# One residual-and-norm hand-over chained, and the differential attention re-staged: query tiles computed inside it, probabilities joined and transposed one step behind their scores and multiplied with v two behind

## The chip, the cores and the metric

The kernel runs on one core of a Trainium2 chip. The metric is the time of one execution on the device in microseconds (us). Before the change three runs took 3192.56, 3198.44 and 3200.86 us; the median is 3198.44.

## The reference, cut to what matters

Two models run one after the other on 512 tokens of width 1024. The first has two layers (gated linear attention, then S5), each closed by an output projection added to `x`, and ends in a norm. The second puts 16 meta tokens in front (528 tokens, `L2`) and has an even layer (RWKV beside pooling), an MLP, an odd layer (differential attention) and an MLP. Two places matter here.

The seam between the models: `x = rms_norm(x, final_norm_w)` on the 512 tokens, and at once `h = rmsnorm([meta; x], norm_g_2[0][0])` on all 528, which feeds the even layer's input projection. `x` itself stays the residual.

The differential attention has 8 heads. Each head has two components c = 0, 1 of 64 dimensions and a value of 128. Rotary embedding is applied to q and k. Then:

```
s_c = causal(q_c k_c^T / 8),  p_c = softmax(s_c)           c = 0, 1
o   = (p_0 - lam * p_1) v          lam from four 64-vectors
o   = rms(o over 128) * subln * (1 - LAM_INIT),  then od_out
```

The last 512 tokens are queries, all 528 are keys.

## The kernel before, in words

Nothing is scheduled by a planner. Each stage is an object with methods `tensor`, `scalar`, `vector` and `gpsimd`, and each engine runs the stages' methods in the order in which they are appended; semaphores alone tie the engines together. The order of instructions on each engine is thus the order of the code.

Matrix products with weights (`Gemm`, L101) stream units of 128 x 1024 weights through a ring of four slots, loaded by SyncE. ScalarE rounds a unit to `high` (L362), GpSimd subtracts it from the unit to give the rest, `ring_r` (L353), and TensorE makes three products per 128 x 128 block: high weight by high input (L260), high by rest (L263), rest by high (L265). An output tile of 512 tokens is 24 matmuls of 512 columns; one of 528 tokens is 48 of 264.

The seam. `Rms` after out1 (built at L3183) gathers squares of `x` while out1 runs (`square` L512 on ScalarE, `add` L525 on VectorE), sums them over partitions with `ones` (L562, L566), takes the root (L547) and its reciprocal (L584), and scales `x` in place (L592). The second `Rms` (`pre(0, 0, rms)`, L3286) squares the new `x` tile by tile (L542), sums with 32 matmuls (L572), takes root and reciprocal again, writes `h` (L592), its rounding (L553) and its rest (L597); the first product of ev_a waits for the first rest. `RwkvPrepare` and `Rwkv` follow; in `Rwkv` GpSimd does only L2191.

The odd layer. `LateRms` (L609) lets the first output tile of the following product run in plain fp32 on unnormalised input (L246) and brings the statistic later. Then come, one after the other, all 8 query tiles (`RopeProjection`, 512 tokens), all 8 key tiles (528 tokens), `TokenInverse`, the values `gv` (four token tiles of 128 and one of 16), and `DiffAttention` (L2498). Rotary work per tile: four ScalarE copies of 32 rows (L2461, L2462), then three VectorE operations (L2491, L2493, L2495).

`DiffAttention` walks 32 steps n = (head h, query tile tau), with 144, 272, 400 or 528 keys. Its engines run:

- TensorE: scores of n for both components into banks 2(n%2) and 2(n%2)+1 (L2553, L2554; the 16 keys beyond 512 by L2552, L2557), then step n-2's probabilities transposed and combined as `prob_c x diag_c`, two accumulating fp32 products per key tile (L2568), then step n-3's product with v (L2579). All are fp32, and each such matmul appears in the trace as two passes.
- VectorE: adds the mask on the edge tile (L2672), one maximum for both components (L2677); for n-1 the inverse sums (L2691, L2692) and two diagonal matrices 1/sum_0 and lam/sum_1 (L2693, L2694).
- ScalarE: two exponentials with their sums (L2604, L2607), the copy of the transposed probabilities of n-2 (L2617, L2618); once per head the copy of the output (L2625) and four squares (L2639).

A tail makes the norm: root (L2642), diagonal spreads (L2702), products that transpose the output (L2589), its rounding (L2647) and rest (L2706), which feed od_out.

Of the kernel before, what the change touches and what calls it, by code (L numbers as in the profile page):

```python
# [23 lines left out]
P = 128  # L24
D = 1024
# [75 lines left out]
class Gemm(Stage):  # L101
# [13 lines left out]
    def __init__(self, b, name, kind, x, kt, outs, ranges, store, engines, needs, tiles=None, before=None,  # L115
# [10 lines left out]
        self.first_use = {}  # L126
        self.late, plain = late, int(late is not None)
# [28 lines left out]
        if high is not None:  # L156
            assert self.body_units % 2 == 0, name
            b.splits += self.body_units * self.iters - plain
# [48 lines left out]
    def tensor(self, pe):  # L207
# [26 lines left out]
        def one_out(o, it, ks=range(self.kt)):  # L234
# [5 lines left out]
            for c in range(ks[0] // 8, -(-(ks[-1] + 1) // 8)):  # L240
                w = self.unit(pe, it, o * self.per_out + c)
                for k in range(max(8 * c, ks[0]), min(8 * c + 8, ks[-1] + 1)):
# [12 lines left out]
                    if self.high is not None:  # L255
                        if self.ready and o == 0 and isinstance(it, int) and it == 0:
                            pe.wait_ge(*self.ready(k))
                        cols, hi = slice(k % 8 * P, (k % 8 + 1) * P), self.high[:, (o * self.per_out + c) % 2, :]
# [18 lines left out]
        def token_major(it):  # L277
            for j in range(self.body_units):
                w = self.unit(pe, it, j).rearrange("p (k n) -> p k n", k=2)
                for i, (t0, tn) in enumerate(self.tiles):  # L280
                    if j == 0:
                        free(i, it)
                    for kk in range(2):
                        if self.high is not None:
                            hi = self.high[:, j % 2, kk * 512:kk * 512 + 512]
# [63 lines left out]
    def make_low(self, eng, j, it):  # L349

        b, slot = self.b, (self.unit0 + j) % RING
        eng.wait_ge(b.unit_hi, self.split0 + j + 1 + it * self.body_units)
        eng.tensor_tensor(b.ring_r[:, slot, :], b.ring[:, slot, :], self.high[:, j % 2, :],  # L353
                                  ALU.subtract).then_inc(b.unit_lo, 1)

    def make_high(self, act, j, it, free=False):
# [5 lines left out]
        b.nc.scalar.activation(self.high[:, j % 2, :], b.ring[:, u % RING, :], ACT.Copy).then_inc(b.unit_hi, 1)  # L362
# [245 lines left out]

class LateRms(Stage):  # L609
# [79 lines left out]
class TokenInverse(Stage):  # L689


    def __init__(self, b, late, bank, to, turned, kept, before):
        self.b, self.late, self.bank, self.to = b, late, bank, to
        self.turned, self.kept, self.before = turned, kept, before

    def tensor(self, pe):
        b = self.b
        pe.wait_ge(*self.late.inverted)
        for o, (t0, tn) in enumerate(TOK_TILES):
            ins = b.nc.tensor.matmul(b.ps[0:tn, self.bank, o:o + 1], b.inv[:, t0:t0 + tn], b.ident[:, 0:1],  # L700
                                     start=True, stop=True)
        ins.then_inc(self.turned, 1)

    def scalar(self, act):
        act.wait_ge(self.kept, self.before + 2)

    def vector(self, dve):
        n = len(TOK_TILES) - 1
        tn = TOK_TILES[n][1]
        dve.wait_ge(self.turned, self.before + 1)  # L710
        self.b.nc.vector.tensor_copy(self.to[:, 0:n], self.b.ps[:, self.bank, 0:n]).then_inc(self.kept, 1)
        self.b.nc.vector.tensor_copy(self.to[0:tn, n:n + 1], self.b.ps[0:tn, self.bank, n:n + 1]).then_inc(self.kept, 1)
        dve.wait_ge(self.kept, self.before + 2)

# [958 lines left out]
N_CHUNKS = -(-L2 // RW_C)  # L1673
RANGES2 = HALVES
# [185 lines left out]
class Rwkv(Stage):  # L1860
# [323 lines left out]
    def gpsimd(self, pool):  # L2184
        b, m = self.b, self.m
        self.pool.gpsimd_tiles(pool)
        for n in range(self.groups):
            half, nch = n % 2, self.chunks(n // 2)
# [220 lines left out]
class RopeProjection(Stage):  # L2409


    def __init__(self, b, m, g, first, following, sems):
        self.b, self.m, self.g, self.first, self.following = b, m, g, first, following
# [3 lines left out]
        self.done = (self.done_, first + self.tiles)  # L2417
        self.kept = slice(META if len(g.ranges) == 1 else 0, L2)
        self.scale = 0.125 if first == 0 else 1.0
# [13 lines left out]
    def turn(self, n):  # L2433

        return self.m.part[(self.first + n) % 2]
# [14 lines left out]
    def shift(self, act, n):  # L2450

        b, at = self.b, self.first + n
# [12 lines left out]
    def scalar(self, act):  # L2465
# [9 lines left out]
        for n in (self.tiles - 2, self.tiles - 1):  # L2475
            self.shift(act, n)

    def vector(self, dve):
        b, m, v = self.b, self.m, self.b.nc.vector
        if self.first == 0:  # L2480
# [4 lines left out]
        for n in range(self.tiles):  # L2485
            at = self.first + n
            par, full = self.full(n)
            x, t = self.shaped(m.qk(at)), self.shaped(self.turn(n))
            dve.wait_ge(b.filled[par], full)
            dve.wait_ge(self.shifted, at + 1)  # L2490
            v.scalar_tensor_tensor(out=x, in0=self.source(n), scalar=self.scale, in1=cos, op0=ALU.mult,  # L2491
                                   op1=ALU.mult).then_inc(b.stored[par], 1)
            b.chain.link(v.tensor_tensor(t, t, sin, ALU.mult))  # L2493
            dve.wait_ge(b.stored[par], full)
            v.tensor_tensor(x, x, t, ALU.add).then_inc(self.done_, 1)  # L2495


class DiffAttention(Stage):  # L2498
# [4 lines left out]
    def __init__(self, b, m, needs):  # L2503
        self.b, self.m, self.needs = b, m, needs
        self.products = b.sem("da_products")
        self.summed = b.sem("da_summed")
        self.exped = b.sem("da_exped")
        self.scored = b.sem("da_scored")
        self.tail_scored = b.sem("da_tail_scored")
        self.maxed = b.sem("da_maxed")  # L2510
        self.powered = b.sem("da_powered")
        self.scaled = b.sem("da_scaled")
# [3 lines left out]
        self.out_kept = b.sem("da_out_kept")  # L2516
        self.steps = DIFF_HEADS * 4
        self.at = dict(b.norms)
        b.norms["squared"] += self.steps
# [4 lines left out]
        self.feeds = None  # L2524

    def parts(self, n):

        h, tau = divmod(n, 4)
        t0 = META + tau * P
        tiles = [(i * P, P) for i in range(tau + 1)] + [((tau + 1) * P, META)]  # L2530
        return h, tau, slice(t0, t0 + P), t0 + P, tiles

    def tensor(self, pe):
        b, m, mm = self.b, self.m, self.b.nc.tensor.matmul
        for s, v in self.needs:
            pe.wait_ge(s, v)
        pe.wait_ge(self.products, 1)
        mm(b.ps[:, 7, 0:2], b.ones[0:DIFF_DIM, :], m.lam_prod[0:DIFF_DIM, :], start=True, stop=True).then_inc(self.summed, 1)
        for n in range(self.steps + 3):
            if n < self.steps:  # L2540
                h, tau, tok, nk, tiles = self.parts(n)
                main = min(nk, 512)
                if n >= 2:
                    pe.wait_ge(self.powered, 2 * n - 2)
                if nk > main and h:
                    pe.wait_ge(self.kept, 4 * h)
                q = [m.qk(h)[DIFF_DIM * c:DIFF_DIM * (c + 1), tok] for c in range(2)]
                k = [m.qk(8 + h)[DIFF_DIM * c:DIFF_DIM * (c + 1)] for c in range(2)]
                to = [b.ps[:, 2 * (n % 2) + c, 0:main] for c in range(2)]
                tail = [b.ps[:, 6, META * c:META * (c + 1)] for c in range(2)]  # L2550
                if nk > main:
                    mm(tail[0], q[0], k[0][:, main:nk], start=True, stop=True).then_inc(self.tail_scored, 1)  # L2552
                mm(to[0], q[0], k[0][:, 0:main], start=True, stop=True)  # L2553
                ins = mm(to[1], q[1], k[1][:, 0:main], start=True, stop=True)  # L2554
                if nk > main:
                    pe.wait_ge(self.tail_scored, h + 1)
                    ins = mm(tail[1], q[1], k[1][:, main:nk], start=True, stop=True)  # L2557
                ins.then_inc(self.scored, 1)
            if 2 <= n < self.steps + 2:
                j = n - 2  # L2560
                h, tau, tok, nk, tiles = self.parts(j)
                pe.wait_ge(self.scaled, j + 1)
                if j >= 2:
                    pe.wait_ge(self.kept, j - 1)
                for i, (k0, kn) in enumerate(tiles):
                    to = b.ps[0:kn, 4 + j % 2, i * P:(i + 1) * P] if i < 4 else b.ps[0:kn, 6, P:2 * P]
# [978 lines left out]
```

## Time and profile before

| what | value |
|---|---|
| median of three runs | 3198.44 us |
| the profiled execution's own time / its span | 3202.0 / 3200.2 us |
| granted TensorE clock over the span | 0.964 |
| TensorE matmul busy | 2927.9 us, 91% |
| VectorE / ScalarE / GpSimd busy | 1398.6 (44%) / 1008.2 (32%) / 1050.6 (33%) us |
| seam, last add to `x` until first product of ev_a | 1637.7 to 1664.8 us of the span |
| query / key / value products (after the late tile) | 2459.4 to 2506.6 / to 2553.9 / to 2611.0 |
| differential attention, first score to last product with v | 2612.8 to 2742.0 |

TensorE's busy share says little on its own, since its ends are modelled. What a change is worth is read from a stretch: its length, the starts of successive groups on TensorE, and the idle time in brackets with what ended it. The granted clock is 1.0 at 2.4 GHz and 0.5 at 1.2 GHz; a mean between them is a share of time at each.

### The profile page before, as it was taken

To read this page: it belongs to the slowest core of one execution; us is meant where nothing else is said; L and a number is where in the kernel's file an instruction comes from. 1 tells how busy PE (TensorE), PEld (TensorE's weight loads), DVE (VectorE), ACT (ScalarE), POOL (GpSimd) and SP (SyncE) were. 2 spreads that over 40 slices of the span, in tenths; PEclk is the share of its full clock that TensorE was granted. 3 is DMA by queue.
4 is the path that set the end of the run, shared out by engine and by line. 5 is a ranking of instruction groups with operands and counts; after the bars stand their busy time and mean duration, and the time that the engine had idled before them with its cause. 6 is when DMAs were issued, how large, how long until landed. Compare 5 with 4: busy or idle time off the path is not lost. (4 is left out here: it accounts for less than half of the span.)

```text
span 3200.2 us, 45703 instructions
## 1 busy us (share of the span) xinstructions
PE 2927.9 (91%) x18218; PEld 2384.0 (74%) x18218; DVE 1398.6 (44%) x2300; ACT 1008.2 (32%) x1613; POOL 1050.6 (33%) x725
## 2 busy tenths in 40 slices
PE   6898789899899899898979888899998999989997
PEld 4666467677688578786768876799997867768885
DVE  5787254510206511302038575380634425283352
ACT  2222264222312235423225332311124525431121
POOL 0332022444323169444433300144442320234442
PEclk9999899999999899999999997999999999999999
DMA  3898011144472269322222100122222210122222
GB/s 138 259 273 260 22 46 47 59 154 155 150 210 92 80 159 257 117 94 77 93 77 67 41 3 15 60 89 89 93 91 75 86 46 1 47 73 98 92 96 75
DMA packets 130754, 324.91 MB, mean 102 GB/s; under 512 B 54144, under 2 KB 54784, under 8 KB 129808
## 3 DMA queue, kind: packets, MB, share of 16 engines
q1 hardware_dynamic: 96128, 221.90, 21.5%
q0 software_dynamic: 30096, 88.21, 9.8%
q10 hardware_dynamic: 4352, 12.25, 1.0%
q8 instruction: 133, 2.18, 0.3%
q14 instruction: 45, 0.37, 0.0%
HBM read 288.32 MB, written 33.95 MB: 101 GB/s over the span
## 5 line engine op out<-in xcount | busy, mean ns | idle before, releaser
L353 POOL TENSOR_TENSOR ring_r<-ring,high 128x1024 fp32r<-128x1024 f32 x327 | 823.5, 2518 | 1570.6 <-ACT high L362 1570.5
L260 PE MATMUL ps<-h_hi,high 128*128 128x512 f32 (+1 forms) x2112 | 737.8, 358 | 55.0 <-POOL ring_r L353 23.7
L265 PE MATMUL ps<-h_hi,ring_r 128*128 128x512 f32 (+1 forms) x2112 | 663.2, 349 | 0.0
L263 PE MATMUL ps<-h_r,high 128*128 128x512 f32 (+1 forms) x1920 | 646.2, 346 | 0.0
L362 ACT ACTIVATE high<-ring 128x1024 fp32r<-128x1024 f32 x359 | 379.5, 1057 | 831.0 <-PE ps L260 711.0
L260 PEld LDWEIGHTS ps<-h_hi,high 128*128 128x128 f32 x2112 | 402.7, 191 | 133.9 <-issue 61.6
L265 PEld LDWEIGHTS ps<-h_hi,ring_r 128*128 128x128 f32 x2112 | 372.3, 191 | 53.6
L263 PEld LDWEIGHTS ps<-h_r,high 128*128 128x128 f32 x1920 | 367.7, 192 | 42.1 <-issue 1.7
L263 PE MATMUL ps<-f_r,high 128*128 128x264 f32 (+1 forms) x832 | 261.2, 326 | 0.0
L260 PE MATMUL ps<-f_hi,high 128*128 128x264 f32 (+1 forms) x768 | 236.6, 321 | 0.0
L260 PE MATMUL ps<-z_hi,high 128*128 128x512 f32 x488 | 196.6, 403 | 16.7 <-POOL ring_r L353 10.9
L265 PE MATMUL ps<-f_hi,ring_r 128*128 128x264 f32 (+1 forms) x768 | 205.0, 321 | 0.0
L265 PE MATMUL ps<-z_hi,ring_r 128*128 128x512 f32 x488 | 192.4, 394 | 0.0
L263 PEld LDWEIGHTS ps<-f_r,high 128*128 128x128 f32 x832 | 156.8, 188 | 14.4
L2920 ACT ACTIVATE arena<-ps 128x512 f32<-128x512 f32 (+4 forms) x102 | 58.3, 575 | 342.1 <-PE ps L265 251.8
L260 PEld LDWEIGHTS ps<-f_hi,high 128*128 128x128 f32 x768 | 144.4, 188 | 11.4
L263 PE MATMUL ps<-z_lo,high 128*128 128x512 f32 x360 | 145.4, 404 | 0.0
L265 PEld LDWEIGHTS ps<-f_hi,ring_r 128*128 128x128 f32 x768 | 127.0, 188 | 11.0
L3354 DVE CAST f_hi<-f x64 | 131.6, 2056 | 7.8
L260 PEld LDWEIGHTS ps<-z_hi,high 128*128 128x128 f32 x488 | 92.9, 190 | 44.9 <-issue 14.5
L263 PE MATMUL ps<-z_hi,high 128*128 128x512 f32 x280 | 112.5, 402 | 0.0
L265 PEld LDWEIGHTS ps<-z_hi,ring_r 128*128 128x128 f32 x488 | 93.2, 191 | 22.4
(430 smaller groups left out, 4387.6 us busy)
## 6 DMA issues: line engine op xcount, KB each, us to landing
ring<-in_units SPq DMA_DIRECT2D x402, 512.0 KB, 3.3
d_ca<-arena POOLq DMA_DIRECT2D x16, 640.0 KB, 8.7
arena<-d_ca POOLq DMA_DIRECT2D x16, 640.0 KB, 6.0
arena<-d_q POOLq DMA_DIRECT2D x32, 256.0 KB, 7.8
d_pb<-arena POOLq DMA_DIRECT2D x16, 512.0 KB, 10.5
arena<-d_pb POOLq DMA_DIRECT2D x16, 512.0 KB, 4.0
arena<-d_ca POOLq DMA_DIRECT2D x16, 512.0 KB, 5.1
arena<-d_k POOLq DMA_DIRECT2D x128, 64.0 KB, 4.4
```

The source lines that it names most:

```text
L260: part = mm(acc, hi[:, cols], self.x_hi(k)[:, t0:t0 + tn], start=(k == 0), stop=False)
L263: mm(acc, hi[:, cols], self.x(k)[:, t0:t0 + tn], start=False, stop=False)
L265: ins = mm(acc, w[:, cols], self.x_hi(k)[:, t0:t0 + tn], start=False, stop=(k == self.kt - 1))
L353: eng.tensor_tensor(b.ring_r[:, slot, :], b.ring[:, slot, :], self.high[:, j % 2, :], ALU.subtract).then_inc(b.unit_lo, 1)
L362: b.nc.scalar.activation(self.high[:, j % 2, :], b.ring[:, u % RING, :], ACT.Copy).then_inc(b.unit_hi, 1)
L2920: return nc.scalar.activation(to, ps, ACT.Copy, scale=1.0 if scale is None else scale)
L3354: nc.vector.tensor_copy(hi, t).then_inc(mlp_parts, 1)
```

## The change

Seam. One stage `ChainedNorms` replaces both norms. While out1 runs, ScalarE squares each tile twice, plain and scaled by the weight w (with a scale column that `WideColumns` computes once, near the start), and VectorE adds both running sums. TensorE sums the meta tokens' squares and the weighted sums; one root and one reciprocal of these give the factor for `h`, since the second norm of a normed input is, up to its epsilon, a norm of `x * w`. The factor of the first norm is taken later from the plain sums, behind the `h` work, and `x` is brought up to date tile by tile by GpSimd inside `Rwkv`.

Odd layer. New order: 8 key tiles (late tile first), one query tile, `TokenInverse` with lam, values (16 meta tokens now last), then `DiffAttention` with the other 7 query tiles inside. Each step holds two of the eight k-blocks of a query tile, 6 matmuls (`query_tile`). In the attention:

- score bank c is used in every step; component c of step n waits for the exponential c of step n-1; the mask is a third accumulating matmul, `ident_r x hide_r`; the maximum is taken per component;
- `join`: VectorE computes `p_0 - (lam sum_0 / sum_1) p_1` unnormalised in one operation, TensorE transposes it once per key tile, one step behind the scores, and multiplies with v two behind;
- the division by sum_0 moves to the copy of the head's output, now VectorE's (`keep_out`); squares move to GpSimd and their sum to VectorE;
- GpSimd makes the 7 query units' rests, ScalarE their roundings and rotary copies, VectorE their rotary sums, all between attention steps.

Core of the diff (weights reordered to match, and buffers moved):

```diff
+    def scalar(self, act):                      # ChainedNorms
+        act.wait_ge(b.summed, at["summed"] + 1)
+        f(b.root[:, META:], b.ps[:, 0, :], ACT.Sqrt, bias=b.eps[self.eps * self.eps], scale=1.0 / self.width)
+        f(b.root[:, 0:META], b.ps[:, 2, 0:META], ACT.Sqrt, bias=b.eps[self.eps], scale=1.0 / self.width)
+        self.feeds.make_high(act, 0, 0)
...
+    def residual(self, pool, k):                # called by Rwkv.gpsimd before its wait for group k
+        pool.tensor_scalar(x, x, b.col("final_norm_w", k), 1.0, ALU.mult, ALU.mult).then_inc(b.normed, 1)
+        pool.wait_ge(b.normed, at["ready"] + self.n + 2 * k + 1)
+        pool.tensor_tensor(x, x, b.inv[:, META:], ALU.mult).then_inc(b.normed, 1)
...
     # DiffAttention.tensor, step n
-                mm(to[0], q[0], k[0][:, 0:main], start=True, stop=True)
-                ins = mm(to[1], q[1], k[1][:, 0:main], start=True, stop=True)
+                for c in range(2):
+                    to = b.ps[:, c, 0:main]
+                    if n:
+                        pe.wait_ge(self.powered, 2 * n - 1 + c)
+                    mm(to, q[c], k[c][:, first:nk], start=True, stop=False)
+                    mm(to[:, main - P:main], m.ident_r, m.hide_r, start=False, stop=True).then_inc(self.scored, 1)
+                self.query_tile(pe, 4 + 2 * n)
-                j = n - 2
-                pe.wait_ge(self.scaled, j + 1)
-                    for c in range(2):
-                        ins = mm(to, m.prob[:, j % 3, c, k0:k0 + kn], m.diag[:, j % 2, c, :], start=(c == 0), stop=(c == 1))
+                j = n - 1
+                pe.wait_ge(self.joined, j + 1)
+                    ins = b.nc.tensor.transpose(self.turned_to(j, i, kn), m.prob[:, j % 3, 0, k0:k0 + kn], b.ident[:, :])
-                j = n - 3                       # product with v
+                j = n - 2
...
+        def join(j):                            # vector, after the maxima of step j + 1
+            dve.wait_ge(self.powered, 2 * j + 2)
+            link(v.reciprocal(inv, tot))
+            link(ts(inv[:, 1:2], inv[:, 1:2], tot[:, 0:1], m.lam, ALU.mult, ALU.mult))
+            stt(out=p[:, 0], in0=p[:, 1], scalar=inv[:, 1:2], in1=p[:, 0], op0=ALU.mult, op1=ALU.add).then_inc(self.joined, 1)
...
+        for n in range(self.steps + 1):         # scalar
+            power(n); keep(n - 1)
+            if n % 4 == 0: self.q.g.high_unit(act, n // 4 + 1)
+            if n % 4 == 1 and n // 4 < self.q.tiles: self.q.shift(act, n // 4)
...
+        for h in range(DIFF_HEADS):             # gpsimd, after low_unit(0) and low_unit(1)
+            self.q.g.low_unit(pool, h + 2)
+            squares(h)
```

## Rows read from the trace of the kernel before

**Rows 1.** The page, busy time of each engine.
```profile
PE 2927.9 (91%) x18218; PEld 2384.0 (74%) x18218; DVE 1398.6 (44%) x2300; ACT 1008.2 (32%) x1613; POOL 1050.6 (33%) x725
```

**Rows 2.** By stretch: length, busy PE PEld DVE ACT POOL, granted clock, DMA, GB/s.
```profile
1820.00:1860.00 40.00, 34.10 (x995) 30.57 (x995) 21.86 (x59) 13.62 (x35) 3.31 (x3) 1.00 0.01 4
1085.00:1143.00 58.00, 43.56 (x132) 24.97 (x130) 22.93 (x74) 17.27 (x50) 6.76 (x12) 0.82 0.16 46
2459.40:2506.60 47.20, 42.73 (x175) 33.33 (x174) 32.45 (x37) 29.81 (x46) 17.79 (x7) 0.96 0.33 108
2506.60:2553.90 47.30, 46.92 (x385) 46.74 (x384) 18.50 (x25) 27.71 (x40) 19.38 (x8) 1.00 0.28 90
2553.90:2611.00 57.10, 56.84 (x251) 41.39 (x250) 5.43 (x10) 13.14 (x16) 16.81 (x7) 1.00 0.22 74
2612.80:2742.00 129.20, 125.97 (x834) 93.31 (x834) 68.87 (x227) 69.22 (x289) 0.00 (x0) 0.97 0.01 1
```

**Rows 3.** Timeline of the seam: start, us, engine, line, operation, [idle before <-releaser].
```profile
1637.71 1.07 DVE L3173 TENSOR_TENSOR x<-x,ps 128x512 f32<-128x512 f32 x1 [15.07 <-PE ps L265]
1638.70 0.68 DVE L525 TENSOR_TENSOR sq<-sq 128x512 f32<-128x512 f32 x1
...
1639.53 1.10 PE L562 MATMUL ps<-sq,c_ones 128*128 128x512 f32 x2 [1.85 <-DVE sq L525]
1640.46 1.02 PE L566 MATMUL ps<-sq,c_ones 128*128 128x512 f32 x2
1641.52 0.69 ACT L547 ACTIVATE root<-ps,c_eps 128x512 f32<-128x512 f32 x1 [0.77 <-PE ps L566]
...
1658.45 3.45 DVE L584 RECIPROCAL inv<-root 128x528 f32<-128x528 f32 x1 [7.43 <-ACT root L547]
...
1661.93 2.13 DVE L592 SCALAR_TENSOR_TENSOR h<-x,cols,inv 128x528 f32<-128x528 f32 x3
1664.83 0.56 PE L260 MATMUL ps<-h_hi,high 128*128 128x264 f32 x1 [7.30 <-DVE h_r L597]
```

**Rows 4.** Timeline of VectorE behind the seam, in `RwkvPrepare`.
```profile
1681.57 0.15 DVE L1689 TENSOR_SCALAR sq<-arena 128x1 f32<-128x1 f32 x1 [5.29 <-ACT arena L2920]
```

**Rows 5.** Timeline of one head of the attention, TensorE's groups and some of VectorE's.
```profile
2648.31 0.60 PE L2553 MATMUL ps<-arena 64*128 64x400 f32 x1
...
2653.81 1.22 DVE L2677 TENSOR_REDUCE arena<-ps 128x2 f32<-128x1024 f32 x1
...
2659.30 0.49 PE L2553 MATMUL ps<-arena 64*128 64x272 f32 x1
...
2659.97 2.59 PE L2568 MATMUL ps<-arena 128*128 128x128 f32 x20
...
2662.49 1.35 PE L2579 MATMUL ps<-arena 128*128 128x128 f32 x8
...
2663.76 0.60 PE L2553 MATMUL ps<-arena 64*128 64x400 f32 x1
```

**Rows 6.** Groups by line over that head, 2648.31 to 2663.76.
```profile
L2568 PE MATMUL ps<-arena 128*128 128x128 f32 (+1 forms) x56 | 7.7, 282 | 0.1
```

**Rows 7.** Timeline in `Rwkv`: transposes on TensorE, GpSimd's only work.
```profile
1834.83 1.09 PE L1969 MATMUL ps<-c_ident,arena 128*128 128x128 f32 x8
...
1835.51 1.27 POOL L2191 TENSOR_TENSOR arena<-arena,memn 128x512 f32<-128x512 f32 x1 [14.74 <-ACT arena L2084]
```

**Rows 8.** Timeline of a softmax step of the memory attention, TensorE.
```profile
1117.17 0.44 PE L761 MATMUL ps<-c_ident,p 128*128 128x128 f32 x2 [0.98 <-DVE p L797]
1117.44 1.03 PE L742 MATMUL ps<-arena 128*128 128x256 f32 x4
```

**Rows 9.** Timeline at the turn from queries to keys: VectorE and GpSimd.
```profile
2510.32 2.48 POOL L353 TENSOR_TENSOR ring_r<-ring,high 128x1024 fp32r<-128x1024 f32 x1 [5.27 <-ACT high L362]
2510.58 2.77 DVE L2495 TENSOR_TENSOR arena<-arena 128x512 f32<-128x512 f32 x1
```

**Rows 10.** Timeline of TensorE after the last product with v.
```profile
2746.73 3.78 PE L2589 MATMUL ps<-arena 128*128 128x128 f32 x16 [4.74 <-DVE arena L2702]
```

More of the change, by code:

```diff
@@ L704, in scalar @@
[L704 to L713 removed]
+        pe.wait_ge(*self.free)
@@ L1673 @@
 N_CHUNKS = -(-L2 // RW_C)
+KEY_TILES = [(META + t * P, P) for t in range(4)] + [(0, META)]
 RANGES2 = HALVES
@@ L2433, in turn @@
     def turn(self, n):
-        return self.m.part[(self.first + n) % 2]
+        return self.m.part[(self.base + n) % 2]
     def full(self, n):
@@ L2450, in shift @@
     def shift(self, act, n):
-        b, at = self.b, self.first + n
+        b, at = self.b, self.base + n
         par, full = self.full(n)
@@ L2474, in scalar @@
         self.following.make_high(act, 0, 0)
-        for n in (self.tiles - 2, self.tiles - 1):
+        for n in range(max(0, self.tiles - 2), self.tiles):
             self.shift(act, n)
@@ L2524, in __init__, with turned_to @@
         self.feeds = None
+        self.turned_at = turned.base - 1
     def parts(self, n):
         h, tau = divmod(n, 4)
-        t0 = META + tau * P
-        tiles = [(i * P, P) for i in range(tau + 1)] + [((tau + 1) * P, META)]
-        return h, tau, slice(t0, t0 + P), t0 + P, tiles
+        tiles = [(META + i * P, P) for i in range(tau + 1)] + [(0, META)]
+        return h, tau, META + tau * P, META + (tau + 1) * P, tiles
+    def turned_to(self, j, i, kn):
+        b = self.b
+        return b.ps[0:kn, 4 + j % 2, i * P:(i + 1) * P] if i < 4 else b.ps[0:kn, 6, P:2 * P]
@@ L2533, in tensor, with query_tile @@
+    def query_tile(self, pe, n):
+        if n < 8 * self.q.tiles:
+            it, o = divmod(n // 8, self.q.g.body_outs)
+            self.q.g.one_out(o, it, range(n % 8, n % 8 + 2))
     def tensor(self, pe):
         b, m, mm = self.b, self.m, self.b.nc.tensor.matmul
[L2535 to L2538, printed above, removed]
@@ L2611, in keep @@
         def keep(j):
-            h, tau, tok, nk, tiles = self.parts(j)
+            h, tau, t0, nk, tiles = self.parts(j)
             act.wait_ge(self.turned, j + 1)
@@ L2695, in vector @@
+        for n in range(self.steps + 4):
+            if n >= 6 and n % 4 == 2:
+                keep_out(n // 4 - 1)
+            if n < self.steps:
+                top(n)
+            if 1 <= n <= self.steps:
+                join(n - 1)
+            if n % 4 == 2 and n // 4 < self.q.tiles:
+                self.q.combine(dve, n // 4)
+            if n >= 8 and n % 4 == 1:
+                sum_squares(n // 4 - 2)
+        sum_squares(DIFF_HEADS - 1)
         dve.wait_ge(b.rooted, self.at["rooted"] + 1)
@@ L2984, in build @@
         stages.append(rms)
+        wide = Views()
+        columns = b.sb("wide", [P, 2, KD])
+        wide.scale, wide.gain = columns[:, 0, :], columns[:, 1, :]
+        wide.meta = b.h[:, 4, 0:KD * META].rearrange("p (k t) -> p k t", k=KD)
+        stages.append(WideColumns(b, wide))
         memn = lambda k: b.memn[:, k, :]
```

486 lines of the change are left out of this document (299 added, 187 removed).

## The prediction

> **What bounds the kernel now.** I read the page's busy line first: TensorE is busy 91%, no other engine half [rows 1]. So a part pays where it takes work off TensorE or shortens a stretch in which TensorE idles. Next the two stretches that the change touches. At the seam the timeline shows the last add to `x` starting at 1637.71 and the first product of ev_a at 1664.83; between them runs one chain over ScalarE and VectorE, twice (root, reciprocal, scaling), with TensorE only summing squares [rows 3]. In the odd layer, key and value products fill TensorE (46.92 of 47.30, 56.84 of 57.10 us); the query products, which come first, carry start-up losses (42.73 of 47.20); the attention takes 129.20 us with TensorE busy 125.97 [rows 2]. One head of the attention lasts 2663.76 - 2648.31 = 15.45 us [rows 5]. TensorE's program sets that pace; VectorE, ScalarE and GpSimd are busy 69, 69 and 0 of 129 us [rows 2].
>
> **The seam.** The last add ends at 1638.78. After it VectorE adds twice (two L525 of 0.68): 1640.15. TensorE sums the meta squares, 16 short passes; no row shows 16-column passes of this kind, the bounds are near 0 and the 0.12 of a 128-column pass, and since weights change each time I take 0.1: 1.7 us. The weighted sums take what L562 and L566 take now, 1639.53 to 1641.48, 1.95: 1643.8. Root 0.69, a small root and hand-overs 0.35: 1644.85. Reciprocal 3.45: 1648.3. From there the first product starts 1664.83 - 1661.93 = 2.90 after the reciprocal now; three tiles now need an extra 16-column instruction each, 0.1 apiece: 1651.5 [rows 3]. That is 13.3 earlier. The later tiles come every 1.42 instead of 1.30 us for seven tiles, 0.8 back: gain 12.4, bounds 10 and 14.
>
> What it pushes elsewhere: the reciprocal for `x` (3.4 us) stands on VectorE behind the `h` work, ahead of `RwkvPrepare`. VectorE waits 5.29 us there for ev_a's second tile [rows 4], which hides it; with that cover gone it would cost 3.4. The second square and add per tile run beside out1, whose tiles come over 15 us apart (the add waited 15.07) [rows 3]: nothing. The update of `x`, 8 times two GpSimd operations of some 1.27, goes where GpSimd idles 14.74 us between pieces [rows 7]; L2191 waits for ScalarE, not for GpSimd. It can hold up VectorE (see below), bounds 0 and 8 x 1.3 = 10; the operations of VectorE that follow L2191 mostly read PSUM, I take 0.
>
> **The odd layer outside the attention.** Two start-ups change hands. Query stage now: 7 tiles after the late one, 24 matmuls at 0.232 = 5.57 each, 39.0 of 47.2, so 8.2 of start-up loss. Keys run at 47.3/8 = 5.9 with none [rows 2]. After: 7 key tiles 41.1 + the same 8.2 = 49.3; one query tile 5.6; values 57.1 unchanged; a hand-over to the attention 0.7, since two query chunks (2.8 us) cover the constants. lam leaves the start of the attention.
>
> **TensorE's work per head.** Products with diagonals go: 56 passes [rows 6], 20 of them from 2659.97 to 2662.49 at 0.126: 7.1 us. In their place 14 transposes of one pass each. Eight transposes take 1.09 to the end of the last, and the last itself about 0.27: 0.117 apiece [rows 7], so 14 x 0.12 = 1.7. Products with v stay, 28 passes at 0.155 (the 8 from 2662.49 to 2663.76 at 0.159): 4.3 [rows 5].
>
> Scores become dearer. Now the two components use different halves of the array's rows and overlap: 272 columns take 2659.30 to 2659.97, 0.67, for four passes [rows 5]; by that slope the four query tiles of a head take about 3.05. The mask product, on all rows, now stands between c = 0 and c = 1, so they run one after the other. A pass alone: 256 columns on all rows, four in 1.03 [rows 8], 0.24 each, hence 0.15, 0.26, 0.36 and 0.46 for 144 to 512 columns; 16 passes 4.9. Bounds: 4.9, and 6.1 if each keeps its present pace. I take 4.9, the lone pass being the nearer kind. Meta scores 0.4. Masks: 8 products of 128 columns in fp32r; from a full-rate product (0.232 per 512 columns) 0.06, from a whole fp32 product of 128 columns, two passes, 0.25; I take 0.10, nearer the first since it is of that kind, 0.8 per head. Query chunks: 24 x 0.232 = 5.6. Sum with queries 4.9 + 0.4 + 0.8 + 5.6 + 1.7 + 4.3 = 17.7; without them 12.1.
>
> **Gaps on TensorE.** Transposes of n-1 wait for `join`, which VectorE starts only after both maxima of n. So after the scores of n, TensorE has 1.39 us of query chunk, and VectorE needs: hand-over 0.2; maximum of c = 1 (1024 columns take 1.22 [rows 5], so 0.28, 0.40, 0.53 and 0.65, with 0.2 more at tau = 3); two small operations 0.4 (three at a predecessor of 528 keys, 0.6); the joining operation over n-1's keys (528 columns about 0.77; 0.30, 0.45, 0.60 below); hand-over 0.06. Per tau 0 to 3: 1.91, 1.36, 1.64, 2.11, less 1.39: 0.52, 0, 0.25, 0.72.
>
> GpSimd adds one. It had nothing to do in the attention [rows 2]. A VectorE operation with both inputs in SBUF that begins under a GpSimd operation waits for its end: L2495 began 0.26 after a GpSimd start and took 2.77 in place of about 0.7, ending just behind it [rows 9]. By the order of ScalarE's program, rounding of the next query unit ends as step tau = 1 begins, GpSimd's 2.48 follow, and that step's join falls under them: its 0.30 becomes some 1.45, gap 1.12. The squares (1.27) fall under maxima, which read PSUM. Gaps per head: 0.52 + 1.12 + 0.25 + 0.72 = 2.6, a period of 20.3. ScalarE, some 10 us of it, follows.
>
> Head 8 and most of head 7 have no query chunks: 12.1 + 7.0 = 19.1. The whole: lead-in chunks 2.8, first head 16.1 (its first steps have nothing to transpose or multiply), five at 20.3, one at 19.2, the last with its drain 22.5: 162.1.
>
> **The clock.** In `Rwkv` TensorE is busy 34.1 of 40 and the grant is 1.00; in the memory attention, with 0.98 of idle in each step of about 2.3 us [rows 8], 43.56 of 58, it is 0.82 [rows 2]. The last ten steps (some 37 us) have such gaps. At 0.82, 13 us at half speed; TensorE is about 0.62 of the chain, half of that lost: 4 us. Bounds 0 and 15.
>
> The Trainium skill, page "TensorE: Matmul & The Clock Gate", Part 4, says that transpose-mode products don't count as activity for the clock gate. No row here isolates it: the memory attention has both gaps and transposes, `Rwkv` has transposes at a grant of 1.00. If so, the steps without queries would fall sooner; it makes the last rival likelier, and no term above hangs on it.
>
> **Tail.** Now 4.74 us from the last product with v to the next on TensorE [rows 10]. After: scaled copy 0.7, GpSimd squares 1.3, their sum 0.6, root 0.3, reciprocal 0.35, spread 0.7, hand-overs 0.4, 4.3 in all. I count it equal.
>
> **Sum.** Before, 2459.4 to 2742.0 is 282.6. After: 49.3 + 5.6 + 57.1 + 0.7 + 162.1 = 274.8, gain 7.8, less 4 for the clock 3.8. With the seam's 12.4: 16.2. The profiled execution took 3202.0 (span 3200.2), so 3185.8; it stands 3.6 above the median of 3198.4, so 3182.
>
> **Rivals.**
> - *Cheaper attention.* GpSimd doesn't hold up the join (0.87 + more per head, 6.5 in all), the clock holds (4), masks at 0.06 (2): 12.5 better, 3170. For: the attention's TensorE was steady at nearly 1.00. Against: rows 9.
> - *Scores at their present pace.* Each pass keeps 0.24 to 0.52 when alone, 1.2 per head, 7.3 with the knock-on, and masks 0.13 or more, 2 more: 3191. For: short passes carry weight loads. Against: [rows 8].
> - *Slower, the clock.* Gaps in every step, with short and transposing work between, bring the grant down through the whole attention. At the memory attention's 0.82 over 162 us, 58 us run at half speed; half of it lost, 29, less 4 counted: 3207. Fully at 1.2 GHz it would be over 100 more. It decides from 26 us lost. For: [rows 8] at 0.82. Against: query chunks of 1.39 us in 26 of 32 steps, and `Rwkv` at 1.00 with gaps.
> - *The norm hand-over is not worth it*, because VectorE bounds `RwkvPrepare` and starts late: 9 instead of 12.4, 3186; inside the forecast's range.
>
> **How the numbers follow.** A run can tell 0.3%, 9.6 us, from no change: faster is below 3188.8. Forecast 3182 has 0.52 (own range 3175 to 3190), cheaper attention 0.22, present-pace scores 0.16, the clock 0.10. Faster: nearly all of the first two less a tail, 0.69; same, the third and that tail, 0.21; slower 0.10. Range 3162 to 3200: the low end adds the seam's and chunks' upside to the second case, the high end leaves out the clock case.
>
> **What would show it.** Seam: ev_a's first product 13 us closer to the last add, one reciprocal in between. Attention: head period near 20.3 with query chunks and 19 without; transposes at 0.12; score passes of one component not overlapping the other's; the join at tau = 1 stretched under L353; grant near 1 until the last two heads. Wrong if the head period is above 22, if the seam gives under 9, or if VectorE's joins are never stretched.

## The result and the profile after

The changed kernel took 3217.44 us in the median (8 runs), the kernel before 3199.89 beside it: ratio 1.0049, 95% interval 1.0035 to 1.0063. It is slower by half a per cent, where 3182 was forecast with 3162 to 3200 as its range. The profiled execution took 3212.11 (span 3210.3) against 3202.0. One of the 8 runs, a stray of 7313.84 us that nothing here explains, counts in the median (3216.53 without it) but not in the ratio.

The page, busy time of each engine, answers to [rows 1]:

```profile
PE 2932.5 (91%) x17926; PEld 2370.7 (74%) x17926; DVE 1406.5 (44%) x2290; ACT 999.7 (31%) x1521; POOL 1075.2 (33%) x751
```

The trace has 292 passes of TensorE fewer (18218 to 17926) and TensorE is busy 4.6 us longer: the first sign that what was taken off it came back at a higher price. By stretch of the changed kernel (columns as in [rows 2]): `Rwkv`, keys, the first query tile, values, the attention, its last head:

```profile
1820.00:1860.00 40.00, 34.25 (x1004) 30.02 (x997) 26.42 (x67) 15.78 (x36) 9.16 (x9) 1.00 0.01 3
2449.10:2498.60 49.50, 44.95 (x350) 43.51 (x349) 35.53 (x38) 31.45 (x49) 17.31 (x7) 1.00 0.31 105
2498.60:2504.40 5.80, 5.80 (x33) 4.93 (x32) 4.11 (x3) 3.73 (x6) 2.52 (x1) 1.00 0.26 90
2504.40:2561.00 56.60, 56.60 (x246) 41.24 (x245) 5.48 (x12) 15.12 (x20) 19.19 (x8) 1.00 0.22 75
2562.70:2752.70 190.00, 173.47 (x717) 111.30 (x716) 89.34 (x227) 85.28 (x235) 21.54 (x13) 0.86 0.05 18
2713.90:2752.70 38.80, 32.08 (x94) 20.77 (x93) 11.50 (x31) 9.77 (x28) 1.04 (x1) 0.50 0.00 1
```

Keys, first query and values lie where the forecast put them (49.3, 5.6 and 57.1). The attention takes 190 us, and its last row shows a granted clock of 0.50, the lower of TensorE's two levels, 1.2 GHz.

The seam, timeline of the changed kernel, against [rows 3]:

```profile
1636.95 1.07 DVE L3364 TENSOR_TENSOR x<-x,ps 128x512 f32<-128x512 f32 x1 [15.05 <-PE ps L266]
...
1639.27 1.96 PE L661 MATMUL ps<-h,c_ones 128*128 128x16 f32 x16 [2.36 <-DVE sq L654]
...
1644.74 0.27 ACT L675 ACTIVATE root<-ps,c_eps 128x16 f32<-128x16 f32 x1
...
1645.04 3.45 DVE L690 RECIPROCAL inv<-root 128x528 f32<-128x528 f32 x1 [5.82 <-ACT root L675]
...
1651.81 0.56 PE L261 MATMUL ps<-h_hi,high 128*128 128x264 f32 x1 [5.35 <-DVE h_r L700]
```

One reciprocal stands between the last add and the first product; from the start of the one to the start of the other it is 14.86 us, before 27.12.

A steady head of the attention, TensorE's timeline of the changed kernel, step tau = 0 whole, of tau = 1 and 3 the part in question:

```profile
2645.77 0.51 PE L2727 MATMUL ps<-arena 64*128 64x144 f32 x2
2646.21 0.33 PE L2731 MATMUL ps<-z_hi 128*128 128x128 f32 x1
2646.47 0.51 PE L2727 MATMUL ps<-arena 64*128 64x144 f32 x2
2646.91 0.33 PE L2731 MATMUL ps<-z_hi 128*128 128x128 f32 x1
2647.07 0.45 PE L261 MATMUL ps<-h_hi,high 128*128 128x512 f32 x1
...
2648.29 0.39 PE L266 MATMUL ps<-h_hi,ring_r 128*128 128x512 f32 x1
2649.02 0.76 PE L2740 MATMUL ps<-c_ident,arena 128*128 128x128 f32 x5 [0.34 <-DVE arena L2867]
2649.62 1.25 PE L2750 MATMUL ps<-arena 128*128 128x128 f32 x8
2650.80 0.72 PE L2727 MATMUL ps<-arena 64*128 64x272 f32 x2
2651.45 0.33 PE L2731 MATMUL ps<-z_hi 128*128 128x128 f32 x1
...
2665.82 0.66 PE L2740 MATMUL ps<-c_ident,arena 128*128 128x128 f32 x4 [0.58 <-DVE arena L2867]
...
2667.27 0.39 PE L2727 MATMUL ps<-arena 64*128 64x144 f32 x1
```

Read the first five lines from start to start. Two passes of 144 columns for component 0 (0.44), their mask (0.26), two passes for component 1 (0.44), mask (0.16), and only then the query chunk: 1.30 us. In [rows 5] the two components' passes of 272 columns begin together, four in 0.67; here that tile takes 1.72 with its masks. Over the head the scoring blocks are 1.30, 1.72, 2.15 and 2.75, together 7.92 us.

The steps of head 8, which have no query chunk beside them:

```profile
2713.90 0.84 PE L2727 MATMUL ps<-arena 64*128 64x144 f32 x2
...
2718.11 1.33 PE L2740 MATMUL ps<-c_ident,arena 128*128 128x128 f32 x5 [1.78 <-DVE arena L2867]
2719.24 2.21 PE L2750 MATMUL ps<-arena 128*128 128x128 f32 x8
...
2744.06 1.12 PE L2740 MATMUL ps<-c_ident,arena 128*128 128x128 f32 x4 [2.03 <-DVE arena L2867]
...
2756.83 3.79 PE L2760 MATMUL ps<-arena 128*128 128x128 f32 x16 [4.09 <-DVE arena L2888]
```

The same passes take 0.84 where they took 0.51. The last line is the tail, 4.09 against 4.74 [rows 10].

### The profile page after: what moved, and what is told of

It is laid out like the page before. It is cut to its first block and busy times, and to the rows that moved or that the text cites. A ratio compares the mean times of both kernels' runs of the same rounds, so it can differ in the third digit from the quotient of the medians.

```text
span 3210.3 us, 45040 instructions
## 1 busy us (share of the span) xinstructions
PE 2932.5 (91%) x17926; PEld 2370.7 (74%) x17926; DVE 1406.5 (44%) x2290; ACT 999.7 (31%) x1521; POOL 1075.2 (33%) x751
## 3 DMA queue, kind: packets, MB, share of 16 engines
q8 instruction: 131, 2.15, 0.3%
## 5 line engine op out<-in xcount | busy, mean ns | idle before, releaser
L261 PEld LDWEIGHTS ps<-z_hi,high 128*128 128x128 f32 x488 | 93.0, 191 | 49.3 <-issue 14.0
L266 PEld LDWEIGHTS ps<-z_hi,ring_r 128*128 128x128 f32 x488 | 93.1, 191 | 22.3
## 6 DMA issues: line engine op xcount, KB each, us to landing
d_pb<-arena POOLq DMA_DIRECT2D x16, 512.0 KB, 10.7
```

The lines of the kernel that those rows point to most:

```text
L261: part = mm(acc, hi[:, cols], self.x_hi(k)[:, t0:t0 + tn], start=(k == 0), stop=False)
L266: ins = mm(acc, w[:, cols], self.x_hi(k)[:, t0:t0 + tn], start=False, stop=(k == self.kt - 1))
```

## The experiments

Times are medians, ratios are to the kernel before in the same call. "Attention" is measured within each profiled execution, from the first score to the end of the last product with v, so that nothing ahead of it moves it. "Period" is a steady head, from one 144-key score to the next; "head 7 / 8" are the last two heads, the eighth to its last product with v.

```
kernel            median   ratio (95%)             attention  period  head 7 / 8
changed           3217.44  1.0049 (1.0035-1.0063)    190.1    21.50   25.1 / 38.8
seam_only         3188.32  0.9963 (0.9949-0.9977)    129.2    15.46   15.5 / 24.5
odd_only          3218.51  1.0064 (1.0043-1.0086)    188.4    21.51   24.2 / 38.8
no_mask           3188.41  0.9962 (0.9943-0.9981)    166.1    19.42   21.1 / 32.2
filler            3195.90  0.9978 (0.9966-0.9989)    174.0    21.50   21.3 / 24.8
filler_turns      3192.59  0.9977 (0.9961-0.9992)    173.9    21.50   21.3 / 24.7
adjacent          3196.21  0.9979 (0.9964-0.9994)    172.6    19.98   22.8 / 33.6
adjacent_filler   3176.58  0.9920 (0.9896-0.9945)    160.2    19.98   20.1 / 23.9
join_first        3187.67  0.9968 (0.9956-0.9980)    167.2    19.50   17.6 / 32.5
pairs_and_join    3159.96  0.9876 (0.9858-0.9894)    142.0    17.03   16.9 / 26.6
all_three_six     3159.76  0.9881 (0.9861-0.9901)    140.6    17.03   16.9 / 25.3
all_three         3158.57  0.9865 (0.9841-0.9889)    137.9    17.03   17.1 / 22.4
```

**seam_only**: the kernel before with the new norm stage and nothing else of the change.

```diff
-        rms = pre(0, 0, rms)
+        rms = ChainedNorms(b, x2, KD, D, EPS, wide, lambda i: b.h[:, 5 + i, 0:L1], h_hi, h2_lo, h2)
...
+                self.norms.residual(pool, n)
```

> The kernel before with the new norm hand-over alone; the differential attention is the old one. Theory A (the seam saves what its steps saved, 13 us, and 3 to 4 of them go back at the end of Rwkv because the grant falls to 0.50 about 8 us earlier there, counted from the kernel's own place): -9 to -10 us, some 3190. Rival (the seam's 13 us stay whole): -12 to -13, some 3187. Rival (a lower clock eats them all): within 2 us of before. The attention must last as long as before, 293 us from the odd layer's late tile to the last v product.

It is 0.37% faster, 11.8 us of 3200 (the interval is 7.4 to 16.3; the medians differ by 12.6). The attention is as it was (129.2). By the times, Theory A and its first rival differ by 3 us and neither is excluded; that the clock eats the gain is.

The traces do tell them apart. This is the stretch of `Rwkv` at the lower clock, in the kernel before and in the changed one:

```profile
1952.90:1987.00 34.10, 28.53 (x239) 20.70 (x239) 17.64 (x60) 7.95 (x23) 0.91 (x2) 0.50 0.00 1
1932.00:1976.30 44.30, 37.67 (x403) 28.86 (x402) 23.02 (x79) 8.71 (x26) 0.91 (x2) 0.50 0.01 1
```

Counted from the last add to `x`, `Rwkv` begins 164.8 and 164.9 us later in the two kernels with the old norms, and 151.3 to 154.2 in the eleven with the new ones, the changed kernel among them: a lead of 10.6 to 13.6. From there to the late tile of the first MLP it is 253.2 with the old norms. In nine of the eleven it is 256.3 to 256.6, and in those the low stretch lasts 44 us, as here. In the two others (filler_turns, all_three_six) it lasts 34 us as before, and the distance is 253.1. So where the low stretch is longer 3.2 us of the lead go back, as Theory A has it; where it is not, nothing does, which also shows that the update of `x` on GpSimd costs nothing.

**odd_only**: the converse, the new odd layer behind the old norms.

```diff
-        stages.append(RopeProjection(b, m3, gq, 0, None, turns))
...
+        keys = Turned(b, m3, gk, 0, 0, None, turns)
...
-        da = DiffAttention(b, m3, [rope.done, third_in] + done(gv))
+        da = DiffAttention(b, m3, queries, done(gv))
```

> The changed odd layer alone, with the old norm hand-over. If the two parts add up: +21 to +25 us, some 3221 to 3225, and the same fall of the grant to 0.5 once the query chunks have run out, about 25 us before the last v product. If the loss in the attention came from the seam's shift of the clock, the grant stays at 1.0 through the attention here and the time is within 8 us of before.

Slower by 0.64% (0.43 to 0.86), 20.5 us; the attention is that of the changed kernel to 2 us, with the clock falling in the same place, in head 7 soon after the last query chunk. So the whole loss belongs to the odd layer. The two ratios give +0.27% together where the changed kernel has 0.49; each has an interval of 0.14 to 0.22 to either side, so they are not at odds.

**no_mask**: how much is the mask's place worth? The kernel leaves the causal mask out of the computation.

```diff
-                    mm(to, q[c], k[c][:, first:nk], start=True, stop=False)
...
-                    mm(to[:, main - P:main], m.ident_r, m.hide_r, start=False, stop=True).then_inc(self.scored, 1)
+                    mm(to, q[c], k[c][:, first:nk], start=True, stop=True).then_inc(self.scored, 1)
```

> The changed kernel without the mask product, so the scores above the diagonal stay unmasked (left out of the computation: the causal mask). Theory B (the full-row mask product between the two components' scores is what keeps them from running beside each other): the scoring blocks of a steady head fall from 7.9 us to 3.4 to 3.8, the period from 21.5 to about 17.5, and the time by 25 to 35 us against the changed kernel, some 3185. Rival (they run one after the other because each waits for its own component's exponentials): only the masks' own 1.7 us per head go, scoring 6.2, period about 19.8, -12 to -14 us, some 3204.

TensorE's timeline at tau = 0 and 1 of a steady head, with VectorE's and GpSimd's rows of tau = 1:

```profile
2656.18 0.52 PE L2729 MATMUL ps<-arena 64*128 64x144 f32 x4
2656.63 0.51 PE L261 MATMUL ps<-h_hi,high 128*128 128x512 f32 x1
...
2660.47 0.73 PE L2729 MATMUL ps<-arena 64*128 64x272 f32 x4
2661.26 2.38 POOL L354 TENSOR_TENSOR ring_r<-ring,high 128x1024 fp32r<-128x1024 f32 x1 [13.24 <-ACT high L363]
2662.43 1.37 DVE L2865 SCALAR_TENSOR_TENSOR arena<-arena 128x144 f32<-128x144 f32 x1
2663.86 0.44 PE L2738 MATMUL ps<-c_ident,arena 128*128 128x128 f32 x2 [1.07 <-DVE arena L2865]
```

Four passes of 144 columns now take 0.45 and the blocks of a head 3.71 in place of 7.92. Theory B is right about the pairs: they run side by side again, though each component still waits for its own exponentials, so those waits didn't part them. But the period falls by 2.1 and not by 4: TensorE waits 3.1 us a head for the join (0.40, 1.07, 0.47, 1.12) instead of 0.9. The time fell by 0.87%, 28 us, all the same, more than eight times 2.1. Of it the trace shows 24.0 in the attention, 10.7 of them in the last two heads, where the clock is low.

**adjacent**: the same products in another order.

```diff
                 for c in range(2):
...
-                    mm(to, q[c], k[c][:, first:nk], start=True, stop=False)
-                    mm(to[:, main - P:main], m.ident_r, m.hide_r, start=False, stop=True).then_inc(self.scored, 1)
+                    mm(to[c], q[c], k[c][:, first:nk], start=True, stop=False)
+                for c in range(2):
+                    mm(to[c][:, main - P:main], m.ident_r, m.hide_r, start=False, stop=True).then_inc(self.scored, 1)
```

> The changed kernel with the same products in another order: both components' scores first, one behind the other, then both masks. Theory B, with what the run without masks showed (pairs side by side again, 3.4 us a head, but 3.1 us a head of new waits for the join): scoring blocks with their masks 7.9 -> 4.9 to 5.1 us, waits for the join up from 0.9 to about 2.5, period 21.5 -> 19.9 to 20.2, the grant lost as before in the last heads: -10 to -13 us against the changed kernel, some 3205. Rival (the masks' own place keeps pairs apart, whatever the order of the scores): blocks stay at 7.9, period 21.5, no change.

```profile
2641.34 0.73 PE L2727 MATMUL ps<-arena 64*128 64x272 f32 x4
2642.00 0.44 PE L2732 MATMUL ps<-z_hi 128*128 128x128 f32 x2
...
2644.73 0.44 PE L2741 MATMUL ps<-c_ident,arena 128*128 128x128 f32 x2 [0.85 <-DVE arena L2868]
```

Four passes in 0.66, both masks in 0.27: blocks of a head 4.35, less than expected. Waits for the join 3.2, more than expected; the period is 19.98, as expected. Against the changed kernel the ratio fell by 0.70%, 22 us, where 10 to 13 were expected; the attention's own 17.4 are seen in the trace, and 7.6 of these lie in the last two heads, where the clock is low. The rival is out. By the Trainium skill, page "TensorE: Matmul & The Clock Gate", Part 3, products on distinct row groups run side by side. The trace agrees, for pairs that are neighbours, and adds that one full-height product between them parts them. The same page of the Trainium skill, section "Why this matters for your kernels", has a single product of 32 rows take as long as one of 128. No run here has 32 rows; with 64, a lone pass of 272 columns takes 0.33 where a full-height one of 256 takes 0.24 [rows 8], so it is dearer here.

**filler**: is it the clock that makes the last heads long?

```diff
                 self.query_tile(pe, 4 + 2 * n)
+                if n >= 26:
+                    for _ in range(13):
+                        mm(b.ps[:, 3, 0:256], m.ident_r, b.z_hi[:, 22, 256:512], start=True, stop=True)
```

> The changed kernel with 13 products of 256 columns that nobody reads, put where the query chunk stands in steps 26 to 31, in which there is none any more. Theory C (TensorE's granted clock falls to 0.5 because the last steps hold too little work, and that costs about 18 us): the grant stays at 1.0 to the end of the attention, and the time falls by 12 to 18 us against the changed kernel, some 3200 to 3205. Rival (the fall is not what costs: the last heads wait for ScalarE, VectorE and GpSimd anyway): grant 1.0, but at most 3 us back, or the filler's own 1.4 us per step added, +4 to +8.

Windows of the changed kernel and, behind them, of this one:

```profile
2700.00:2720.00 20.00, 14.60 (x45) 8.99 (x45) 8.46 (x22) 6.25 (x21) 0.59 (x1) 0.58 0.00 0
2720.00:2740.00 20.00, 17.10 (x45) 9.94 (x45) 5.21 (x14) 3.62 (x12) 1.04 (x1) 0.50 0.00 0
```

```profile
2700.00:2720.00 20.00, 19.38 (x119) 14.92 (x119) 10.50 (x29) 7.76 (x25) 0.14 (x1) 1.00 0.00 1
2720.00:2740.00 20.00, 15.46 (x89) 11.44 (x88) 10.17 (x24) 7.82 (x19) 3.70 (x3) 0.96 0.00 0
```

Work that nobody reads, 78 products, makes the kernel faster: the attention by 16.0 us with the products' own time paid, the run by 0.71%, 23 us, where 12 to 18 were expected. In the last six steps the grant stays, and Theory C holds. The last two heads alone gained 17.9 us (64.0 to 46.1): this execution has two short dips of the grant in the steady heads, near 2602 and 2684, and the heads in which they fall take 22.5 and 22.3 instead of 21.50.

**filler_turns**: the same with work of another kind.

```diff
+                    for _ in range(12):
+                        b.nc.tensor.transpose(b.ps[:, 3, 0:P], m.o[:, 0, 0, :], b.ident[:, :])
```

> As the changed kernel with the 13 products, but 12 transposes of 128 columns (TensorE's transpose mode, some 1.4 us together by 0.12 each) in their place. The Trainium skill's rule (TensorE: Matmul & The Clock Gate, on transpose mode: it doesn't count as TensorE's activity in the same way): the grant falls to 0.5 as in the changed kernel, time +0 to +12 against it. Rival (work of any kind keeps the grant): as the run with the products, some 3196, grant 1.0 to the last v product.

```profile
2700.00:2720.00 20.00, 18.61 (x116) 13.57 (x115) 10.56 (x29) 7.92 (x26) 0.48 (x1) 1.00 0.00 1
2720.00:2740.00 20.00, 14.95 (x85) 10.74 (x86) 10.44 (x24) 7.83 (x19) 3.42 (x3) 0.89 0.00 0
```

The attention is 173.9, the same to 0.1 us, with two such dips as well. By the Trainium skill, page "TensorE: Matmul & The Clock Gate", Part 4, transpose mode does not count as TensorE's activity in the same way. The trace does not agree, for these fp32 transposes among the steps' other products, with pauses of at most 0.7 us between: the measurement decides.

**adjacent_filler**: the two diffs together.

> Both repairs of the changed kernel: scores adjacent, and the 13 products in steps 26 to 31. If they add: -18 for the grant that stays, -10 to -13 for the pairs: some 3187 to 3190, and about 10 us under the run with the products alone. If the last heads were bound by the join once the clock is high: 3192.

They add: 0.992, and an attention of 160.2. The ratio is 0.58% below filler's, 19 us where 10 were expected; the attention itself gained 13.8.

**all_three**: both, and a swap in VectorE's program. It looks at the waits that `adjacent` laid bare.

```diff
+            if 1 <= n <= self.steps:
+                join(n - 1)
             if n < self.steps:
                 top(n)
-            if 1 <= n <= self.steps:
-                join(n - 1)
```

> Scores adjacent, 13 products in steps 26 to 31, and VectorE joins the step before (L2867) before it takes the maxima of this one (L2852) instead of behind them. Theory D (what is left of the period above TensorE's own work is the join queued behind the maxima, which wait for this step's scores): the waits at L2740 go, period 20 -> 17 to 18, time -15 to -25 against the run without the swap, some 3168. Rival (the maxima, later by the join's 0.7 to 1.3 us, make the next step's scores late by as much): within 3 us of the run without the swap, the wait now stands at the scores L2727, for ScalarE's exponentials.

```profile
2653.22 0.51 PE L2727 MATMUL ps<-arena 64*128 64x144 f32 x2
2653.99 0.51 PE L2727 MATMUL ps<-arena 64*128 64x144 f32 x2 [0.26 <-ACT arena L2783]
2654.43 0.44 PE L2732 MATMUL ps<-z_hi 128*128 128x128 f32 x2
...
2656.15 0.71 PE L2744 MATMUL ps<-c_ident,arena 128*128 128x128 f32 x5
```

No wait stands at the transposes (L2744); part of it has moved to the scores, as the rival said. At tau = 0 the second pair comes 0.77 after the first, for ScalarE's exponentials, so the two no longer run side by side, and the block takes 1.48 from start to start against 0.72 in `adjacent`; at tau = 3 it is 1.92 against 1.55. That is 1.1 us a head, of which the idle column shows 0.26. Period 17.03, ratio 0.9865, 18 us below adjacent_filler. This kernel beats both: 1.35% (interval 1.1 to 1.6) under the kernel before, some 43 us, and 1.8% under the changed one.

**join_first, pairs_and_join, all_three_six**: the swap alone; the swap with adjacent scores, nothing filled in; and all three with `range(6)` in the place of `range(13)`.

```diff
-                    for _ in range(13):
+                    for _ in range(6):
```

> The changed kernel with VectorE's swap alone (join of the step before, then the maxima), pairs apart, nothing filled in. Theory D with pairs apart: a steady head has only 0.9 us of waits for the join to lose (21.5 -> 20.6), the last ten steps lose 1.3 to 2.0 each where the grant is low: -15 to -22 us against the changed kernel, some 3198. Rival (the maxima, late by a join, move the wait to the scores): period 21.5, within 4 us of the changed kernel.

> All but the filled-in products: scores adjacent, join ahead of the maxima. Theory E (the grant falls in the last steps because of TensorE's pauses for the join, and those are gone): grant 1.0 through most of the attention, and the time is that with the products less their own 6 x 1.4 us = 8, some 3150. Theory C (it falls for want of query chunks, pauses or not): grant 0.5 from about step 27, +6 to +14 against the run with the products, 3165 to 3172.

> As the run with all three, with 6 products per step in place of 13 (0.8 instead of 1.8 us a step). If 6 keep the grant: -4 to -6 against it, some 3154. If the grant falls: +6 to +14, and then how much stands in a step is what decides.

The swap alone gives back 0.81%, 26 us (1.0049 to 0.9968), where 15 to 22 were expected; the attention shows 22.8 of them. The steady head lost 2.0, not 0.9: the profile's idle column starts from the modelled end of the last product of the chunk, so its [0.34] stands for 0.50 (start to start 0.73 ahead of the transposes, against 0.23 with the swap). A stall read from that column is a lower bound.

pairs_and_join lands between its theories: the grant falls from about 2680 even with the pauses gone, but for less long, and the attention is 4 us longer than with the products (142.0 against 137.9). So taking the pauses away shortens the low stretch and does not end it. Six products give 140.6, with the grant at 0.50 from 2694 on. In the medians the three can't be told apart (3158.6, 3160.0, 3159.8): once the chain is short, the filled-in work costs about what the clock gives back.

## Why the prediction was wrong

**The profiled execution first.** 3185.8 was forecast for it and it took 3212.1, 26.3 more. The attention is 26.8 over, the seam gave 2.9 less than forecast, and the rest of the odd layer, the stages ahead of the seam and those behind the attention gave 1.9, 0.8 and 0.6 more. Another 9 us of the miss in the median are no part of the kernel: the forecast took the profiled execution to lie 3.6 above the median, as it did before, and here it lies 5.3 below.

**Seam: right at the seam, 3 us given back later.** 13.3 us earlier was forecast for the first product, 12.3 came (10.8 to 12.3 in the eleven traces with the new norms), the meta sums taking 1.96 instead of 1.7 and the weighted sums longer; the later tiles came each 1.43 apart, and by the end of `RwkvPrepare` the lead, counted from the last add, was 12.42, forecast 12.4. The extra reciprocal (1659.96, 3.34 us) hid as said; the wait of [rows 4] is now 2.27, one tile later. What the forecast didn't have is the longer stretch at the lower clock in `Rwkv` (under seam_only): at the odd layer the lead is 9.5.

**Outside the attention: right**, 2 us better than worked out: from the late tile to the first score 124.0 us where the forecast's terms give 125.9. (Seven key tiles at the forecast's own 47.3/8 are 41.4, not 41.1.)

**Attention: wrong by 26.8 us.** From first score to last v product the forecast had 16.1 + 5 x 20.3 + 19.2 + 22.5 = 159.3, and 4 for the clock, 163.3; it took 190.1 (18.6, five times 21.5, 25.1 and 38.8). Against the 159.3 the first six heads are 8.5 over, 2.5 in the first and 1.2 in each steady one, and the last two 22.2. Two terms failed, and the clock's is the larger.

- *"A pass alone ... 0.15, 0.26, 0.36 and 0.46 ... I take 4.9, the lone pass being the nearer kind."* The loss of the overlap was seen, its price was not. A lone pass takes 0.22, 0.33, 0.43 and 0.53 (0.44, 0.65, 0.86, 1.05 for two): the slope per column was right, but each is 0.07 dearer than worked out from the full-height passes of [rows 8], and lasts as long as it did beside another one in [rows 5]. With masks at 0.26 and 0.16 instead of 0.10 the blocks were 7.92 instead of 6.1 (4.9 scores, 0.4 meta, 0.8 masks). Of these 1.8 us a head, smaller waits took back some 0.8. It was the rival "scores at their present pace", given 0.16. Removing it (filler to adjacent_filler) is worth 13.8 us of the attention.
- *"The clock ... 4 us. Bounds 0 and 15."* Mending it gave 16.0 back with the filled-in work's own time paid (changed to filler), so it cost more than the upper bound: the grant went to 0.50 and stayed, not to the 0.82 of the memory attention. The place was right in kind but the count was not: query chunks end with step 25, so six steps are without, not ten, and head 7's first two steps still have theirs. The grant fell at 2703.4, within the first step without (it begins at 2698.68). The depth came from a stretch in which the grant swung back. And a low clock does not only stretch TensorE's half: each step is one chain (scores, maxima, exponentials, join, transposes), the part on TensorE doubles, and pauses of 1.3 to 2.0 us appear between. The clock rival, given 0.10, had the low clock, spread over the whole attention; it was confined to these six steps.

With the two repaired the attention takes 160.2 us, the filled-in products' own time in it, against the forecast's 159.3 at a full clock. The close fit is partly luck, since that is another kernel than the one forecast: its blocks take 4.35 where the forecast had 6.1, and its waits are larger than the forecast's 2.6 (period 19.98 against 20.3).

**Gaps: right in kind.** Forecast 0.52, 1.12, 0.25, 0.72 for tau 0 to 3; start to start they were 0.50, 0.23, 0.31, 0.75. At tau = 1 the join fell under GpSimd for its last 0.4 us only and was stretched from 0.37 to 0.55:

```profile
2651.59 2.37 POOL L354 TENSOR_TENSOR ring_r<-ring,high 128x1024 fp32r<-128x1024 f32 x1 [15.30 <-ACT high L363]
2653.58 0.55 DVE L2867 SCALAR_TENSOR_TENSOR arena<-arena 128x144 f32<-128x144 f32 x1
```

The slow scores had made it late. With the pairs mended the forecast stretch appears: 1.37 us, and TensorE waits 1.07, in the run without masks. What the forecast didn't ask is whether the wait had to be there: with the join ahead of the maxima it is gone, and in the traces that is the largest single repair (22.8 us of the attention on its own, against 17.4 and 16.0).

**The signs of being wrong were blind to it.** None of the three came true (head period 21.5, not above 22; a seam of 9.5; a join stretched, if by little). All look at the seam and the steady heads, and most of the miss lies in the last two heads.

**What stays open.** The late tile of the first MLP begins anywhere from 2036 to 2054 in the eleven profiled executions with the new norms and at 2053 and 2056 with the old ones, mostly because the last add to `x` itself comes anywhere from 1628 to 1646. Counted from that add, the lead at the late tile is 7.4 to 13.1, 9.5 in the mean. What draws the fall of the grant in `Rwkv`, and why its low stretch is longer in nine of eleven, wasn't tried. Nor was it tried how little would hold the last six steps at 1.00 while their pauses stand: six products a step were tried only with the pauses gone.

## What to carry to other kernels

Passes on half of the array's rows are cheap only in neighbouring pairs: put nothing of full height between two of them, and collect such products behind. When a step of a chain is queued behind one that waits for newer data, ask whether it can go first; here that order on VectorE was worth 22.8 us of the attention in the traces, more than either other repair (in the times the three are 0.81, 0.71 and 0.70%, within each other's intervals). When a filler of useful work runs out before its loop does, look at the granted clock of the steps that are left: they can run at half speed, and then even work that nobody reads can be cheaper than none. Once the pauses were gone it bought nothing measurable. When you list what would show a forecast wrong, include the place where its least certain term acts.

## What the runs showed of the hardware

- Two fp32 components of 64 rows side by side: 144 columns in 0.45, 272 in 0.66, 400 in 0.87 for four passes (no_mask); one after the other the two take 0.88, 1.30 and 1.72 without their masks (changed kernel). The pair is worth a factor of two within 3%, and it comes back with the order alone (adjacent).
- A mask product of 128 fp32r columns took 0.26 between passes of half height, 0.16 between such a pass and a full-height query product, and 0.14 apiece with another of its kind beside it.
- Transposes keep the grant as products do: 1.00 and 0.89 against 1.00 and 0.96 in the two windows from 2700 to 2740 (the fall in the second begins near 2736, with the attention over).
- In the last head the grant stayed at 0.50 with TensorE busy 32.1 of 38.8 us (83%); in `Rwkv` it was 1.00 with 34.3 of 40 (86%). Two stretches of nearly the same busy share ran at the two levels. 78 products that nobody reads kept the steps of the last head at 1.00 until the attention was over.
- A short dip of the grant costs a steady head about a microsecond: 22.5 and 22.3 us instead of 21.50, in filler and in filler_turns.
